# Attention groups of w_in ahead of the retention groups, and finished retention rows transposed by VectorE by way of HBM

## The chip, the cores and the metric

One core of one Trainium2 chip runs the whole kernel. The metric is device time in microseconds (us) of that core, the median of several runs. TensorE is called PE, VectorE DVE, ScalarE ACT, GpSimd POOL, and SyncE SP.

## What is computed

The reference is a network on 256 tokens of width 1024 in fp32: two layers of a first block (DEPTH = 2), then two mixers of a second block. The change touches the mixer of the first block's layers alone:

```python
def hybrid_layer(x, g_mix, w_in, sinks, w_a, w_b, w_out, g_mlp, w_up, w_down):
    h = rmsnorm(x, g_mix)
    z = h @ w_in
    aq, ak, av, rq, rk, rv, rg, ga, gb = jnp.split(z, SPLIT_POINTS, axis=-1)
    aq = rope_half(aq.reshape(B, S, N_Q_HEADS, HEAD_DIM), pos)
    ...
    ya = sliding_window_sink_attention(aq, ak, av, sinks) @ w_a
    rq = retention_rotation(rq.reshape(B, S, RET_HEADS, RET_QK_DIM), pos)
    ...
    r = chunkwise_retention(rq, rk, rv)
    r = r * lax.rsqrt(jnp.mean(r * r, axis=-1, keepdims=True) + EPS)
    r = r.reshape(B, S, RET_V) * jax.nn.silu(rg.astype(jnp.float32))
    yb = r.astype(x.dtype) @ w_b
    mixed = jax.nn.sigmoid(ga) * ya + jax.nn.sigmoid(gb) * yb
    x = x + mixed @ w_out
    h2 = rmsnorm(x, g_mlp)
    x = x + jnp.square(jax.nn.relu(h2 @ w_up)) @ w_down
    return x
```

## The kernel before

Each engine has a program written out by hand, and semaphores join them; each engine works its list strictly in order. The tokens are two tiles of 128 rows (t = 0 and 1).

**Weights** come in pieces of 4 x 128 rows by 512 columns (1 MB; 256 columns for the group AKV). SP loads piece p into one of four raw slots as soon as the piece that used the slot, p-4, is split. A product in fp32 is made of three: ACT writes the rounded upper part (w_hi, `split`, L1485), DVE the remainder (w_lo, L1873). Three slots hold split pieces, so ACT splits p only after PE has used p-3; `step(q)` on ACT and DVE stands for splitting piece q+2. PE's `tokens_out` makes one group of output columns from two pieces into PSUM banks 0 and 1 (OUT, one for each token tile); a bank may be written again when ACT or DVE has evacuated it (`out_free`).

**The twelve groups of w_in** are numbered; group g uses pieces 2g and 2g+1. Before, the order is RQ, RK (retention queries and keys), AQ (attention queries), AKV (attention keys and values), RV0, RV1, RG0, RG1, GA0, GA1, GB0, GB1. In layer 0 the first two groups have programs of their own, `first_group` and `second_group`. Then w_a (pieces A, used for YA), w_b (pieces B, YB), w_out and the MLP follow.

**Windows.** Behind each group g, `window(l, g)` on each engine does what small work of attention and retention has come due: scores of a pair of heads, the turn of probabilities, the products with the values, the retention scores s_ret and s_far, the retention outputs. DVE's `softmax(l, i)` (L1947 to L1966) with ACT's exponentials in its middle serves PE's turn in the next window. On PE the window of group g stands behind the group; ACT and DVE do theirs in round g+1, between the two splits of that round. RG0 and RG1 are evacuated by ACT (tanh) and then DVE (L2131), at the end of their round.

**Rotations.** DVE rotates token tile 0 and POOL tile 1, `rotate_pairs` (L576 to L586) for retention and `rotate_halves` (L600 to L611) for attention. `between` puts a split into the middle of DVE's rotation.

**The trip through HBM.** Rotated rows must be transposed. SP stores them to HBM in one piece (`store_rows`), fetches 32-row blocks on other partitions (`fetch_blocks`), and one DVE instruction transposes all 32 x 32 blocks (`turn_blocks`, L1983). `blocks_moved(l, piece)` places these DMAs in SP's queue behind the load of the given piece. Before, r (the retention rows) goes first and a (the attention rows) later, in two stores.

**The finished retention rows** h_sb (DVE L1977) are transposed before by PE: `turn_rows(h, ...)` (L984), between YA and YB. ACT and DVE then bring them from PSUM into hT_hi and hT_lo.

**turn_vectors** runs once, in layer 0: two small PE transposes, the second of which needs dt_rows, spread by a DVE copy (`spread_dt`, L1937).

## Time and profile before

| | before |
|---|---|
| median of 3 runs | 1015.31 us (1014.49 to 1015.38) |
| profiled execution, its own time | 1015.0 us |
| its span, first to last instruction | 1013.1 us |
| granted TensorE clock, mean | 0.998 |
| PE busy | 1004.5 us (99%) |
| DVE, ACT, POOL busy | 720.8 us (71%), 502.3 us (50%), 170.7 us (17%) |
| HBM read and written | 180.69 MB, 4.72 MB |
| chain that ended last | 93% PE, 3% DVE, 1% each DMA, ACT, issue |

All times within the profile are microseconds from the span's start. Busy shares say who works; whether a wait costs anything is told by what PE does meanwhile. Layer 0 of the first block begins at 0, its layer 1 at about 393 us.

### The profile page before, as it was taken

The numbers are of one execution on the slowest core, as the hardware profiler recorded it, in microseconds if no ns is written. First come the engines' busy times: TensorE is split into PE (matmuls) and PEld (weight loads), VectorE is DVE, ScalarE is ACT, GpSimd is POOL, SyncE is SP. The second block draws the span as 40 slices with busy tenths as digits, with TensorE's granted clock in tenths as the row PEclk, the third lists the DMA queues.
The fourth block names the chain that finished last, engine by engine and source line by source line (L and its number), as shares of the span: only waits on it lengthen the run. The fifth ranks groups of instructions, "written<-read, shape, count | busy, mean of one in ns | idle before, by whom it ended". The sixth has DMA issues, their size and how long they took to land.

```text
span 1013.1 us, 13575 instructions
## 1 busy us (share of the span) xinstructions
PE 1004.5 (99%) x5653; PEld 850.0 (84%) x5653; DVE 720.8 (71%) x817; ACT 502.3 (50%) x616; POOL 170.7 (17%) x129
## 2 busy tenths in 40 slices
PE   9999999999999999999999999999999999999997
PEld 8887788888888888887788888888887899899796
DVE  5878656766565665787765667888877757789974
ACT  6544554454444545454554454444468545654352
POOL 0520000000000000430000020000000149169730
PEclk9999999999999999999999999999999999999999
DMA  9797444555556455596553557555554754345451
GB/s 341 250 288 246 160 155 142 170 180 191 199 176 207 166 178 175 187 294 225 166 167 125 169 147 283 201 177 209 204 170 135 238 178 167 125 166 141 121 188 41
DMA packets 103644, 188.60 MB, mean 186 GB/s; under 512 B 9160, under 2 KB 18464, under 8 KB 103456
## 3 DMA queue, kind: packets, MB, share of 16 engines
q1 hardware_dynamic: 103408, 187.66, 55.8%
q8 instruction: 44, 0.72, 0.3%
q14 instruction: 16, 0.13, 0.0%
q10 hardware_dynamic: 176, 0.09, 0.0%
HBM read 180.69 MB, written 4.72 MB: 183 GB/s over the span
## 4 chain that ended last, share of the span: by engine, by line
PE 93%; DVE 3%; DMA 1%; issue 1%; ACT 1%; SPq 0%; DVEq 0%; ACTq 0%
PE bank L786 13%; PE bank L789 12%; PE bank L788 12%; PE bank L1091 11%; PE bank L811 8%; PE bank L815 7%; PE bank L822 7%; PE bank L1095 6%; PE bank L1173 2%; DVE w_lo L1873 2%; PE bank L984 1%; PE bank L1397 1%; PE bank L968 1%; DMA a_bounce<-arena 1%; PE bank L793 1%; PE bank L803 1%
## 5 line engine op out<-in xcount | busy, mean ns | idle before, releaser
L1873 DVE TENSOR_TENSOR w_lo<-arena,w_hi 128x2048 fp32r<-128x2048 f32 (+1 forms) x80 | 185.1, 2323 | 95.2 <-ACT w_hi L1485 94.8
L1873 DVE TENSOR_TENSOR w_lo<-raw,w_hi 128x2048 fp32r<-128x2048 f32 (+1 forms) x78 | 181.1, 2331 | 80.1 <-ACT w_hi L1485 80.0
L1485 ACT ACTIVATE w_hi<-raw 128x2048 fp32r<-128x2048 f32 (+1 forms) x83 | 157.1, 1892 | 102.3 <-PE bank L789 71.4
L1485 ACT ACTIVATE w_hi<-arena 128x2048 fp32r<-128x2048 f32 (+1 forms) x80 | 151.3, 1892 | 104.6 <-PE bank L789 80.8
L1091 PE MATMUL bank<-hT,w_hi 128*128 128x512 f32 x504 | 123.4, 391 | 0.0
L786 PE MATMUL bank<-w_hi,hT 128*128 128x512 f32 (+1 forms) x296 | 114.1, 385 | 0.9 <-issue 0.9
L1091 PEld LDWEIGHTS bank<-hT,w_hi 128*128 128x128 f32 x504 | 92.2, 188 | 17.6
L2482 POOL TENSOR_TENSOR rstd<-mean,const 128x1 f32<-128x1 f32 (+1 forms) x16 | 9.1, 579 | 528.5 <-DVE mean L1882 359.4
L789 PE MATMUL bank<-w_hi,hT 128*128 128x512 f32 (+1 forms) x256 | 97.9, 382 | 0.0
L788 PE MATMUL bank<-w_lo,hT 128*128 128x512 f32 (+1 forms) x256 | 97.9, 382 | 0.0
L811 PE MATMUL bank<-w_hi,hT 128*128 128x512 f32 (+1 forms) x216 | 83.3, 388 | 0.7 <-DVE arena L2131 0.7
L815 PE MATMUL bank<-w_hi,hT 128*128 128x512 f32 (+1 forms) x216 | 82.0, 382 | 0.0
L786 PE MATMUL bank<-w_hi,uT_hi 128*128 128x512 f32 x192 | 74.9, 390 | 0.0
L789 PE MATMUL bank<-w_hi,uT_lo 128*128 128x512 f32 x192 | 74.7, 389 | 0.0
L788 PE MATMUL bank<-w_lo,uT_hi 128*128 128x512 f32 x192 | 74.7, 389 | 0.0
L1095 PEld LDWEIGHTS bank<-hT,w_lo 128*128 128x128 f32 x504 | 67.0, 191 | 3.9
L1095 PE MATMUL bank<-hT,w_lo 128*128 128x256 f32 x504 | 68.3, 282 | 0.0
L786 PEld LDWEIGHTS bank<-w_hi,hT 128*128 128x128 f32 x296 | 55.6, 188 | 12.3 <-DVE w_lo L1873 1.3
L811 PE MATMUL bank<-w_hi,uT_hi 128*128 128x512 f32 x160 | 62.9, 393 | 0.0
L815 PE MATMUL bank<-w_hi,uT_lo 128*128 128x512 f32 x160 | 62.5, 391 | 0.0
L822 PE MATMUL bank<-w_lo,hT 128*128 128x512 f32 (+1 forms) x216 | 56.1, 381 | 0.0
L788 PEld LDWEIGHTS bank<-w_lo,hT 128*128 128x128 f32 x256 | 48.1, 188 | 9.4
(342 smaller groups left out, 1886.7 us busy)
## 6 DMA issues: line engine op xcount, KB each, us to landing
arena<-in_w_in SPq DMA_DIRECT2D x22, 1024.0 KB, 5.3
raw<-in_w_in SPq DMA_DIRECT2D x20, 1024.0 KB, 5.3
arena<-in_w_up SPq DMA_DIRECT2D x16, 1024.0 KB, 5.3
raw<-in_w_up SPq DMA_DIRECT2D x16, 1024.0 KB, 5.3
arena<-in_w_down SPq DMA_DIRECT2D x16, 1024.0 KB, 5.1
raw<-in_w_down SPq DMA_DIRECT2D x16, 1024.0 KB, 5.1
raw<-in_e_w_in SPq DMA_DIRECT2D x6, 1024.0 KB, 5.1
arena<-in_e_w_in SPq DMA_DIRECT2D x6, 1024.0 KB, 5.1
```

Of the source, the lines that this page charges most:

```text
L786: pe.matmul(dst, a_hi, b_hi, start=first, stop=False, skip_group_check=shared)
L788: pe.matmul(dst, a_hi, b_lo, start=False, stop=False, skip_group_check=shared)
L789: mm = pe.matmul(dst, a_lo, b_hi, start=False, stop=last_one, skip_group_check=shared)
L793: pe.matmul(dst, a_hi, b_lo, start=False, stop=False, skip_group_check=shared)
L811: pe.matmul(dst, a_hi, b_hi, start=(start and i == 0), stop=False, skip_group_check=shared)
L815: pe.matmul(dst, a_lo, b_hi, start=False, stop=False, skip_group_check=shared)
L822: mm = pe.matmul(dst, a_hi, b_lo, start=False, stop=last_one, skip_group_check=shared)
L1091: pe.matmul(UP[j], w_hi[:, s[i], kk, at[j]], hT[:, k, :, :].rearrange("p e t -> p (e t)"), start=(i == kk == 0), stop=False, skip_group_ch ...
L1095: return pe.matmul(UP[j][:, 0:SEQ], w_lo[:, s[i], kk, at[j]], hT_hi[:, i * KP + kk, :], start=False, stop=(i == 1 and kk == KP - 1), skip_ ...
L1173: last = pe.matmul(OUT[t], a[:, KP * i + k, at[t]], w[:, s[i], k, :], start=(first and k == 0), stop=(last_one and k == KP - 1))
L1485: act.activation(w_hi[:, p % SPLIT_RING, :, 0:n], raw_at(p)[:, :, 0:n], copy).then_inc(hi_ready, 1)
L1873: dve.tensor_tensor(w_lo[:, s, :, 0:n], raw_at(p)[:, :, 0:n], w_hi[:, s, :, 0:n].bitcast(F32), ALU.subtract).then_inc(lo_ready, 1)
```

## The change

Four things. (1) The order of the groups of w_in becomes AQ, AKV, RQ, RK, RV0 and so on; the tables of the attention's rotation are loaded ahead of the rest, POOL and DVE rotate attention first, and a is stored and fetched first (one store), r later. (2) The windows move: attention starts in window 4, where it started in 6, the retention scores go to windows 6 to 8 and the retention outputs to windows 8 and 9; some PSUM banks change. turn_vectors moves one group later. (3) The finished retention rows are stored to HBM behind the load of w_b's first piece, fetched in blocks behind its second, and transposed by one DVE instruction, which reads every eighth element (`across`). PE's turn_rows(h) goes, and hT_hi and hT_lo are made from SBUF. (4) The rows of w_b are loaded in the matching order (`across_piece`: each partition takes neighbouring rows). In the diff, cut to its core, ACT's windows and PE's turn and value products, each shifted by two groups, are left out.

```diff
-RQ, RK, AQ, AKV, RV0, RV1, RG0, RG1, GA0, GA1, GB0, GB1 = range(12)
-W_IN_START = (768, 1280, 0, 512, 1792, 2304, 2816, 3328, 3840, 4352, 4864, 5376)
+AQ, AKV, RQ, RK, RV0, RV1, RG0, RG1, GA0, GA1, GB0, GB1 = range(12)
+W_IN_START = (0, 512, 768, 1280, 1792, 2304, 2816, 3328, 3840, 4352, 4864, 5376)
...
+ATT_TABLES = ("att_cos", "att_sin")
...
+        h_moved = area(0, T * BLOCKS, KD * BLOCK)
+        h_raw = area(13312, KD, SEQ)
+        h_bounce = nc.dram_tensor("h_bounce", [T * P, D], F32, kind="Internal").ap()
...
+        def across_piece(w, c, half):
+
+            return w.rearrange("(p k) n -> p k n", p=P)[:, half * KP:half * KP + KP, c * COLS:(c + 1) * COLS]
+
...
 def rotate_halves(eng, o, l, t, tmp, between=lambda part: None):
...
+            between(0)
             o.mark(eng.tensor_tensor(b4[:, :, 0, :], z[:, :, 1, :], sin, ALU.mult))
             o.mark(eng.tensor_tensor(b4[:, :, 1, :], z[:, :, 0, :], sin, ALU.mult))
+            between(1)
             o.settle()
...
+                if n[0] == 3:
+                    sp.dma_start(const[:, FIRST_TABLES:SECOND_TABLES], consts[:, FIRST_TABLES:SECOND_TABLES]).then_inc(att_tables, 16)
                 if n[0] == 4:
                     small_inputs()
-                    sp.dma_start(const[:, FIRST_TABLES:], consts[:, FIRST_TABLES:]).then_inc(const_landed, 16)
+                    sp.dma_start(const[:, SECOND_TABLES:], consts[:, SECOND_TABLES:]).then_inc(const_landed, 16)
...
-                if piece == 12:
+                if piece == 10:
+                    for t in range(T):
+                        sp.wait_ge(rope_done[t], l + 1)
+                    store_rows(a_bounce.rearrange("(t p) n -> p t n", p=P), a_rows, a_stored)
+                if piece == 11:
+                    sp.wait_ge(a_stored, 16 * (l + 1))
+                    fetch_blocks(a_moved, a_bounce, a_blocks)
+                if piece == 13:
                     for t in range(T):
                         sp.wait_ge(rot_done[t], l + 1)
                     store_rows(r_bounce.rearrange("(t p) n -> p t n", p=P), z_ret, r_stored)
-                if piece == 13:
+                if piece == 15:
                     sp.wait_ge(r_stored, 16 * (l + 1))
                     fetch_blocks(r_moved, r_bounce, r_blocks)
-                if piece == 14:
-                    sp.wait_ge(rope_done[0], l + 1)
-                    store_rows(a_bounce[0:P, :], a_rows[:, 0, :], a_stored[0])
-                if piece == 15:
-                    sp.wait_ge(rope_done[1], l + 1)
-                    store_rows(a_bounce[P:2 * P, :], a_rows[:, 1, :], a_stored[1])
-                    for t in range(T):
-                        sp.wait_ge(a_stored[t], 16 * (l + 1))
-                        fetch_blocks(a_moved[:, t * BLOCKS:(t + 1) * BLOCKS, :], a_bounce[t * P:(t + 1) * P, :], a_blocks)
...
-                            load(square_piece(ins[w][l], c, half))
+                            load((across_piece if w == "w_b" else square_piece)(ins[w][l], c, half))
+                            if w == "w_b" and c == half == 0:
+                                sp.wait_ge(r_ready, 2 * l + 2)
+                                store_rows(h_bounce.rearrange("(t p) n -> p t n", p=P), h[:, :, :], h_stored)
+                            if w == "w_b" and c == 0 and half == 1:
+                                sp.wait_ge(h_stored, 16 * (l + 1))
+                                fetch_blocks(h_moved, h_bounce, h_blocks)
...
+                width = AKV_WIDTH
...
-                                last = pe.matmul(OUT[t], a[:, i * KP + kk, at], w[:, s, kk, :],
+                                last = pe.matmul(OUT[t][:, 0:width], a[:, i * KP + kk, at], w[:, s, kk, 0:width],
...
             def window(l, g):
-                if l == 0 and g == 1:
+                if l == 0 and g == 2:
                     turn_vectors()
-                if g == 5:
-                    pe.wait_ge(rT_ready, l + 1)
+                if g == 4:
+                    pe.wait_ge(aT_ready, l + 1)
                     if l == 0:
                         pe.wait_ge(vec_ready, 3)
-                    for n in range(T):
-                        at = slice(n * P, (n + 1) * P)
-                        for hd in range(RET_HEADS):
-                            last = pe.matmul(bank[:, 3 + n, hd * P:(hd + 1) * P], rkT[:, hd, at], rqT[:, hd, at],
-                                             start=True, stop=True)
-                        last.then_inc(s_ret_done, 1)
-                if g == 6:
-                    pe.wait_ge(s_ret_ready, 2 * l + 1)
+                if g in (6, 7):
+                    n = g - 6
+                    if n == 0:
+                        pe.wait_ge(rT_ready, l + 1)
+                    else:
+                        pe.wait_ge(s_ret_ready, 2 * l + 1)
+                    at = slice(n * P, (n + 1) * P)
+                    for hd in range(RET_HEADS):
+                        last = pe.matmul(bank[:, 3, hd * P:(hd + 1) * P], rkT[:, hd, at], rqT[:, hd, at], start=True, stop=True)
+                    last.then_inc(s_ret_done, 1)
+                if g == 8:
...
-                    pe.wait_ge(aT_ready, l + 1)
-                if 6 <= g < 6 + PAIRS:
-                    i = g - 6
+                if 4 <= g < 4 + PAIRS:
+                    i = g - 4
...
-                if g == 10:
+                if g == 8:
...
-                if g == 11:
+                if g == 9:
+                    pe.wait_ge(s_far_ready, l + 1)
                     for hd in range(RET_HEADS):
-                        if hd == 2:
-                            pe.wait_ge(oT_lo, l * PAIRS + PAIRS)
-                        dst = bank[:, (4, 3)[hd // 2], (hd % 2) * RET_V:(hd % 2 + 1) * RET_V]
+                        dst = bank[:, (2, 5)[hd // 2], (hd % 2) * RET_V:(hd % 2 + 1) * RET_V]
...
-                           banks_free=lambda: pe.wait_ge(probsT_odd, l * PAIRS + PAIRS))
-                turn_rows(h, lambda t: r_ready, lambda t, i: 2 * l + t + 1)
+                           banks_free=lambda: pe.wait_ge(r_ready, 2 * l + 2))
...
 def group_out(l, g):
-                if g == RQ:
+                if g == AQ:
...
-                window(l, W_IN_GROUPS - 1)
                 step(p + PIECE_A)
+                act.wait_ge(piece_used, p + 2 * W_IN_GROUPS)
+                act.wait_ge(turned, 4 * (4 * l + 1) + 4)
+                for i in range(4):
+                    act.activation(hT_hi[:, 2 * i:2 * i + 2, :], h_raw[:, 2 * i:2 * i + 2, :], copy).then_inc(turned_hi, 1)
                 step(p + PIECE_A + 1)
-                turn_hi(4 * l + 1)
...
+            def turn_blocks(dst, src, slots, across=False):
+
+                rows_in = src.rearrange("p u (f s) -> p u s f" if across else "p u (s f) -> p u s f", s=slots)
+                return dve.transpose(dst.rearrange("p s (u q) -> p u s q", q=BLOCK), rows_in)
             def window(l, g):
                 if g == 1:
+                    dve.wait_ge(att_tables, 16)
+                    rotate_halves(dve, order, l, 0, z_ga, between=lambda part: step(l * PIECES + 5 + part))
+                if g == 3:
                     dve.wait_ge(const_landed, 16)
-                    dve.wait_ge(sink_landed, 16)
-                    dve.wait_ge(vec_ready, 3)
-                    rotate_pairs(dve, order, l, 0, z_ga, between=lambda part: step(l * PIECES + 2 * AQ + 1 + part))
-                if g == 3:
-                    rotate_halves(dve, order, l, 0, z_ga)
-                if g == 5:
-                    dve.wait_ge(aT_ready, l + 1)
-                    for n in range(T):
-                        dve.wait_ge(s_ret_done, 2 * l + n + 1)
-                        dve.tensor_tensor(s_ret[:, n, :], bank[:, 3 + n, :], tab("decay"), ALU.mult).then_inc(s_ret_ready, 1)
-                if g == 6:
+                    rotate_pairs(dve, order, l, 0, z_ga, between=lambda part: step(l * PIECES + 8 + part))
+                if g in (6, 7):
+                    n = g - 6
+                    dve.wait_ge(s_ret_done, 2 * l + n + 1)
+                    dve.tensor_tensor(s_ret[:, n, :], bank[:, 3, :], tab("decay"), ALU.mult).then_inc(s_ret_ready, 1)
+                if g == 8:
                     dve.wait_ge(s_far_done, l + 1)
                     dve.tensor_tensor(s_far, bank[:, 3, :], tab("decay_far"), ALU.mult).then_inc(s_far_ready, 1)
-                if 7 <= g < 7 + PAIRS:
-                    n = l * PAIRS + g - 7
...
-                if 6 <= g < 6 + PAIRS:
-                    softmax(l, g - 6)
-                if g == 10:
-                    retention_out(l, 0)
+                if g == 4:
+                    dve.wait_ge(sink_landed, 16)
+                if 4 <= g < 4 + PAIRS:
+                    softmax(l, g - 4)
+                if g in (8, 9):
+                    retention_out(l, g - 8)
 
...
                     if g == 4:
-                        window(l, g - 1)
+                        dve.wait_ge(a_blocks, 16 * BLOCKS * (l + 1))
+                        turn_blocks(aT, a_moved, A_SLOTS).then_inc(aT_ready, 1)
+                        dve.wait_ge(aT_ready, l + 1)
                     if g == 6:
-                        dve.wait_ge(a_blocks, 16 * T * BLOCKS * (l + 1))
-                        turn_blocks(aT, a_moved, A_SLOTS).then_inc(aT_ready, 1)
-                    if g == 5:
                         dve.wait_ge(r_blocks, 16 * BLOCKS * (l + 1))
                         turn_blocks(rT, r_moved, 2 * RET_HEADS).then_inc(rT_ready, 1)
-                    if g != AKV and (l or g):
+                    if g not in (3, 4) and (l or g):
                         step(p + 2 * g)
-                    if l == 0 and g == 1:
+                    window(l, g - 1)
+                    if l == 0 and g == 2:
                         spread_dt()
-                    if g != 4:
-                        window(l, g - 1)
-                    if g != AQ:
+                    if g not in (2, 4):
...
-                window(l, W_IN_GROUPS - 1)
+                dve.wait_ge(h_blocks, 16 * BLOCKS * (l + 1))
+                turn_blocks(h_raw, h_moved, KD, across=True).then_inc(turned, 4)
                 for c in range(2):
                     step(p + PIECE_A + c)
                     if c == 0:
-                        retention_out(l, 1)
+                        dve.wait_ge(piece_used, p + 2 * W_IN_GROUPS)
+                        for i in range(4):
+                            dve.wait_ge(turned_hi, 4 * (4 * l + 1) + i + 1)
+                            dve.tensor_tensor(hT_lo[:, 2 * i:2 * i + 2, :], h_raw[:, 2 * i:2 * i + 2, :],
+                                              hT_hi[:, 2 * i:2 * i + 2, :].bitcast(F32), ALU.subtract).then_inc(turned_lo, 1)
                     for t in range(T):
                         gated(c, z_ga, l * USES + USE_YA + c, t, banks=(OUT, YA_BANKS)[c])
-                turn_lo(4 * l + 1)
                 for c in range(2):
...
-            pool.wait_ge(const_landed, 16)
-            pool.wait_ge(vec_ready, 3)
+            pool.wait_ge(att_tables, 16)
             for l in range(DEPTH):
+                rotate_halves(pool, order, l, 1, z_gb)
+                if l == 0:
+                    pool.wait_ge(const_landed, 16)
+                    pool.wait_ge(vec_ready, 3)
                 rotate_pairs(pool, order, l, 1, z_gb)
-                rotate_halves(pool, order, l, 1, z_gb)
```

On DVE, in layer 0, round 2 (the group after the second), the change puts the rotation of the attention rows; L1896 is w_lo of pieces 4 to 9, in order, L613 to L626 is rotate_halves, and L1960 is the copy that turn_vectors needs. Before, at the same place:

```order
L1873 TENSOR_TENSOR w_lo<-arena,w_hi 128x2048 [waits hi_ready]
L1873 TENSOR_TENSOR w_lo<-raw,w_hi 128x2048 [waits hi_ready]
L1937 COPY dt_rows<-log_dt 16x128 [waits ldt_landed]
L1873 TENSOR_TENSOR w_lo<-raw,w_hi 128x2048 [waits hi_ready]
L1873 TENSOR_TENSOR w_lo<-arena,w_hi 128x4x256 [waits hi_ready]
```

And now:

```order
L1896 TENSOR_TENSOR w_lo<-raw,w_hi 128x2048 [waits hi_ready] x2
L1896 TENSOR_TENSOR w_lo<-arena,w_hi 128x2048 [waits hi_ready]
L613 TENSOR_TENSOR arena<-arena,const 128x640 [waits out_free0,att_tables]
L1896 TENSOR_TENSOR w_lo<-arena,w_hi 128x2048 [waits hi_ready]
L617 TENSOR_TENSOR arena<-arena,const 128x10x32
L618 TENSOR_TENSOR arena<-arena,const 128x10x32
L1896 TENSOR_TENSOR w_lo<-raw,w_hi 128x2048 [waits hi_ready]
L624 TENSOR_TENSOR arena<-arena 128x4x2x32 [waits dve_order]
L626 TENSOR_TENSOR arena<-arena 128x64 x2
L624 TENSOR_TENSOR arena<-arena 128x4x2x32
L626 TENSOR_TENSOR arena<-arena 128x64 x2
L1960 COPY dt_rows<-log_dt 16x128 [waits ldt_landed,rope_done0]
```

The copy stood between pieces 4 and 5; it now stands behind piece 8 and the end of the rotation.

On ACT, in layer 0, the second group's evacuation (two rows of L1518) stands behind the w_hi of pieces 4 and 5 as the second group's did before, but it is now AKV's:

```order
L1506 ACTIVATE w_hi<-raw 128x2048 [waits piece_used,raw_landed0,half_ready]
L1506 ACTIVATE w_hi<-raw 128x2048 [waits piece_used,raw_landed1]
L1518 ACTIVATE arena<-bank,rstd 128x256 [waits out0_done]
L1518 ACTIVATE arena<-bank,rstd 128x256 [waits piece_used]
L1506 ACTIVATE w_hi<-arena 128x2048 [waits piece_used,raw_landed2]
```

On DVE, rounds 5 and 6 of a layer (behind RV0 and RV1): w_lo of piece 13, then the transpose of r (L2007), piece 14 and the second softmax, which begins at L1970.

```order
L1896 TENSOR_TENSOR w_lo<-raw,w_hi 128x2048 [waits hi_ready]
L2007 STREAM_TRANSPOSE arena<-arena 128x8x8x32 [waits r_blocks]
L1896 TENSOR_TENSOR w_lo<-arena,w_hi 128x2048 [waits hi_ready]
L2028 COPY arena<-bank 128x384 [waits probs_turned]
L1970 SCALAR_TENSOR_TENSOR arena<-bank,const 128x384 [waits probs_turned,scores_done]
L1970 SCALAR_TENSOR_TENSOR arena<-bank,const 128x384
```

Before, both transposes stood ahead of every softmax of the layer:

```order
L1983 STREAM_TRANSPOSE arena<-arena 128x8x8x32 [waits r_blocks]
L1873 TENSOR_TENSOR w_lo<-raw,w_hi 128x2048 [waits hi_ready] x2
L1983 STREAM_TRANSPOSE arena<-arena 128x8x6x32 [waits a_blocks]
L1873 TENSOR_TENSOR w_lo<-arena,w_hi 128x2048 [waits hi_ready]
L1997 TENSOR_TENSOR arena<-bank,const 128x512 [waits s_ret_done,aT_ready]
L1997 TENSOR_TENSOR arena<-bank,const 128x512 [waits s_ret_done]
L1873 TENSOR_TENSOR w_lo<-arena,w_hi 128x2048 [waits hi_ready]
L2131 SCALAR_TENSOR_TENSOR arena<-arena,bank 128x512 [waits tanh_ready] x2
```

The transpose of r moved from ahead of a's to behind the first softmax.

## Rows read from the trace of the kernel before

**Rows 1.** The page, busy time and share of the span by engine.

```profile
PE 1004.5 (99%) x5653; PEld 850.0 (84%) x5653; DVE 720.8 (71%) x817; ACT 502.3 (50%) x616; POOL 170.7 (17%) x129
```

**Rows 2.** Timeline of ACT, layer 1: start, duration, line; evacuations of tile 1.

```profile
415.10 0.69 ACT L1497 ACTIVATE arena<-bank,rstd 128x512 f32<-128x512 f32 x1 [2.03 <-PE bank L789]
...
425.98 0.69 ACT L1497 ACTIVATE arena<-bank,rstd 128x512 f32<-128x512 f32 x1 [2.03 <-PE bank L789]
...
431.73 0.48 ACT L1497 ACTIVATE arena<-bank,rstd 128x256 f32<-128x256 f32 x1 [0.54 <-PE bank L789]
```

**Rows 3.** Chain that ended last, windows of layer 0: start, duration, what.

```profile
69.58 1.78 PE bank L1015 x16
...
109.09 0.81 PE bank L1051 x6
```

**Rows 4.** The same chain, layer 1, between YA and YB.

```profile
548.95 1.75 PE bank L984 x16
550.69 0.46 issue
```

**Rows 5.** Timelines of SP (stores) and of DVE (block transposes), both layers.

```profile
48.13 0.37 SPq L671 DMA_DIRECT2D r_bounce<-arena  x1
...
62.57 0.67 SPq L671 DMA_DIRECT2D a_bounce<-arena  x1
...
432.03 0.37 SPq L671 DMA_DIRECT2D r_bounce<-arena  x1
...
63.79 2.31 DVE L1983 STREAM_TRANSPOSE arena<-arena 128x2048 f32<-128x2048 f32 x1 [1.67 <-DMA arena<-r_bounce]
...
75.58 1.78 DVE L1983 STREAM_TRANSPOSE arena<-arena 128x1536 f32<-128x1536 f32 x1 [5.11 <-DMA arena<-a_bounce]
...
448.87 2.31 DVE L1983 STREAM_TRANSPOSE arena<-arena 128x2048 f32<-128x2048 f32 x1 [2.86 <-DMA arena<-r_bounce]
```

**Rows 6.** Timeline of DVE, layer 0: rotate_pairs beside POOL.

```profile
33.54 3.42 DVE L576 TENSOR_TENSOR arena<-arena,const 128x1024 f32<-128x1024 f32 x1
...
39.35 2.01 DVE L579 TENSOR_TENSOR arena<-arena,const 128x512 f32<-128x512 f32 x1
```

**Rows 7.** Chain that ended last, layer 0: the second group.

```profile
19.52 11.17 PE bank L968 x48
```

**Rows 8.** Timeline of ACT, layer 0: w_hi of pieces 4 and 5, second group's evacuation.

```profile
25.49 1.92 ACT L1485 ACTIVATE w_hi<-raw 128x2048 fp32r<-128x2048 f32 x1 [3.74 <-issue]
28.09 1.92 ACT L1485 ACTIVATE w_hi<-raw 128x2048 fp32r<-128x2048 f32 x1 [0.68 <-DMA raw<-in_w_in]
29.92 1.50 ACT L1497 ACTIVATE arena<-bank,rstd 128x512 f32<-128x512 f32 x2
```

**Rows 9.** Timeline of DVE, layer 0: second half of rotate_halves, and what follows.

```profile
54.75 0.85 DVE L609 TENSOR_TENSOR arena<-arena 128x256 f32<-128x256 f32 x1
...
57.62 4.49 DVE L1873 TENSOR_TENSOR w_lo<-arena,w_hi 128x2048 fp32r<-128x2048 f32 x2
```

**Rows 10.** Timeline of DVE, layer 1: rotate_pairs beside POOL and without it.

```profile
419.33 2.54 DVE L576 TENSOR_TENSOR arena<-arena,const 128x1024 f32<-128x1024 f32 x1
...
430.71 0.69 DVE L585 TENSOR_TENSOR arena<-arena 128x512 f32<-128x512 f32 x1
```

**Rows 11.** Timeline of DVE, layer 1: first softmax and the split behind it.

```profile
471.52 1.01 DVE L1947 SCALAR_TENSOR_TENSOR arena<-bank,const 128x384 f32<-128x384 f32 x2
...
476.56 1.01 DVE L1966 TENSOR_SCALAR arena<-arena,inv_den 128x128 f32<-128x128 f32 x4
477.95 2.29 DVE L1873 TENSOR_TENSOR w_lo<-arena,w_hi 128x2048 fp32r<-128x2048 f32 x1 [0.39 <-ACT w_hi L1485]
```

**Rows 12.** A stretch: busy time by engine, clock, DMA share, GB/s.

```profile
442.00:444.00 2.00, 2.00 (x10) 1.67 (x9) 2.00 (x2) 1.36 (x2) 0.00 (x0) 1.00 1.14 195
```

**Rows 13.** Line 891, keep_clock: count, duration ns min/median/max, first and last start.

```profile
L891 PE MATMUL bank<-h_sb x18: 421/421/579, 1.0 to 4.8; 128*128 128x128 f32 x18
...
L891 PE MATMUL bank<-const x4: 275/275/275, 6.7 to 7.0; 128*128 128x128 f32 x4
```

71 lines of the change are left out of this document (38 added, 33 removed).

## The prediction

> **What bounds the kernel now.** I read the engines' busy shares first: PE is busy for 99% of the span, VectorE (DVE) for 71%, ScalarE (ACT) for 50% [rows 1]. So the end is PE's work plus every hole in it, and before there are hardly any. Hence two questions: what PE work goes, and where a reordered DVE or ACT now leaves PE without input. For that I use how one w_in group passes. ACT's evacuations of the second row tile of successive groups start 10.88 us apart for a group of 512 columns, 5.75 us for the 256 columns of AKV [rows 2]. The four small attention or retention parts placed between groups cost 0.8 to 0.9 us each (transposes 0.81; scores of one retention tile half of 1.78) [rows 3].
>
> Splitting a weight piece takes ACT 1.91 us (w_hi) and then DVE 2.29 us (w_lo). ACT may start on piece p only when PE has used piece p-3.
>
> **What is saved.** In each layer turn_rows(h) disappears from PE: 16 transpose records, 1.75 us, and the 0.46 us gap behind them [rows 4], 2.21 us; two layers give **-4.4 us**. In their place the h rows go through HBM. That trip has two long groups plus the w_a products to hide in, about 11 + 11 + 11 us, after r_ready, which comes some 5 us into GB0. It needs a store and fetch like that of r (15.7 us between store issue and DVE's transpose in layer 0, 16.8 us in layer 1 [rows 5]), then a 2.3 us transpose, four ACT copies and four DVE subtracts (about 5 us): about 29 of 33 us. I cost it at nothing; the strided read of `across` has no row, and if it ran at the slowest rate of a DVE tensor operation here (512 elements in 2.01 us [rows 6]), it would take 8 us and cost up to 3 us per layer. AKV as second group changes PE's total by nothing.
>
> **Start of layer 0: AKV's evacuation.** Before, the second group starts at 19.5 us [rows 7]. AKV will end at 19.5 + 5.8 = 25.3. The next group needs OUT bank 0, so it waits for AKV's evacuation, which on ACT stands behind the w_hi of piece 5. Piece 5 is bound by its load: pieces 4 and 5 are split at 25.49 and 28.09, which are their landings, 2.6 us per MB [rows 8]. Two half-sized pieces ahead of them save 1 MB, so piece 5 lands at 28.1 - 2.7 = 25.4; w_hi ends at 27.3, the 256-column evacuation at 27.7. PE waits **+2.4 us**.
>
> **Start of layer 0: dt_spread.** turn_vectors now follows RQ and needs dt_spread. On DVE that small copy stands behind the whole rotate_halves, whose last part stands behind w_lo of piece 8. Piece 8 can be split only after PE has used piece 5, that is after RQ. From RQ's end: evacuation 0.65, w_hi 1.85, w_lo 2.3, the second half of the rotation 2.87 (start to start beside POOL [rows 9]; POOL will be done, and I take 2.4), copy 0.2, together **+7.4 us** (6.9 to 7.9). There is no such hole before, because the copy is then a DVE instruction between pieces 4 and 5. PE resumes at about 46.
>
> **Each layer: the serial chain to RG1.** Before, DVE turns r for the window after RV1 and a for the one after RG0, and softmax starts only then. Now DVE must, in one line: wait for a's blocks, turn, rotate retention pairs, store and fetch r, turn, then do the second softmax; only after that comes RG0's evacuation, for which RG1 waits. From the end of rotate_halves:
> - a through HBM: 13.0 us (from the second store's issue to DVE's transpose [rows 5]), turn 1.7;
> - rotate_pairs with pieces 10 and 11 between: 3.4 + 2.3 + 4.0 + 2.2 + 1.3 beside POOL in layer 0 [rows 6]; in layer 1 the first multiply still meets POOL (2.5 [rows 10]) and the rest does not (1.2 for the two next multiplies, 0.69 us each [rows 10]), so 9.5;
> - r through HBM 15.7, turn 2.2, w_lo of piece 14 2.2, probsT 0.5, softmax 6.0 (471.5 to 477.6 [rows 11]), w_lo of piece 15 with its gap 2.6, evacuation 0.6: 29.8.
>
> The sum is 57.7 us in layer 0 and 54.0 us in layer 1. PE's own work over that stretch: in layer 0 from RQ's end and the resumption RK, RV0, RV1 and RG0 (43.5 us) with windows 4 to 6 (0.85 + 1.7 + 3.35 = 5.9), 49.4; the chain started 0.3 us earlier, so PE comes **+8.0 us** late. In layer 1, counted from AQ's start, the rotation ends at about 34.7 (RQ ends at 27.5, plus the 7.2 of the paragraph before) and RG1's bank is free at 88.7; PE alone would be there at 16.6 + 54.4 + 5.9 = 77.0: **+11.7 us**. It shows as waits at windows 4 and 5 and, mostly, at window 6. From then on a DVE round is about 13.3 us (two w_lo, softmax, small copies, evacuation) against PE's 14.2, so the lag isn't repeated, nor recovered.
>
> The unsure term is the HBM trips. Bounds: a from 11 us (one larger store without the second one's wait) to 16.8; r from 14 to 16.8 or somewhat more. While r's blocks come back, the DMA engines are full (share 1.14) at only 195 GB/s [rows 12]. The Trainium skill, "DMA: Bandwidth & Descriptors", opening table, has 512 bytes suffice for line rate; by that the 1 KB packets of the blocks would cost half, and the sum would be about 9 us less over four trips. The row disagrees, and it decides.
>
> **Sum:** -4.4 + 2.4 + 7.4 + 8.0 + 11.7 = +25.1 us. The profiled execution took 1015.0 us around a span of 1013.1, the median of the runs is 1015.3; so about **1040 us**. SP's queue: its waits for a's and r's rotations stand ahead of the loads of pieces 11 and 14, which PE needs over 15 us later, so the queue costs nothing. POOL rotates tile 1 beside DVE and ends before it.
>
> **Rivals.**
> 1. *All of it is covered, and the kernel is faster.* The trips return in time and only the transposes go: 1015.0 - 4.4 = 1010.6. For it: PE is 99% busy, and DVE is idle for some us before both transposes. It decides at window 6: the chain would have to be 12 us shorter in layer 1, and dt_spread would still be in the way. 0.05.
> 2. *Only the start is lost.* Both trips together are 8 to 12 us shorter, nothing is late at window 6: 1015.0 - 4.4 + 2.4 + 7.4 = 1020.4. Against it: four measured trips, none under 13 us. 0.08. A draw near 1015 (half of these) 0.03.
> 3. *The clock falls.* The first 18 records of PE's warm-up matmuls have 421 ns, the same shape a few us later 275 ns [rows 13]: PE begins at 1.2 GHz and is at 2.4 some 5 us later, so that stretch once more costs 2.5 us. After the wait for dt_spread it would hide in the chain. After the 5 us wait of window 6 it would not: 2 x 2.5, 1045. The Trainium skill, "TensorE: Matmul & The Clock Gate", section on the HAM clock gate, has the clock fall after an idle stretch; this profile has no stretch with PE idle for over 1.1 us, so it isn't seen here. 0.28.
> 4. *The h blocks are late too* (the slow strided transpose, 8 us): YB waits up to 3 us per layer, about 1045. 0.10.
>
> **How the numbers follow.** Forecast 0.46 at 1040; its own bounds (trips -3 to +3 us per layer, waits at the start +-1) give 1033 to 1048. Clock and h take the top to 1051; the low end goes down to 1029 for shorter trips than any measured. Faster by over 0.2% (2 us, about what a measurement of this kernel can tell) 0.05, within it 0.03, slower 0.92.
>
> **What would show it.** In the changed profile: a PE wait of 7 us after RQ of layer 0, ended by DVE's dt_rows copy; one of 2 to 3 us before RQ, ended by ACT's AKV evacuation; in both layers DVE idle before both block transposes, a PE wait of 4 to 5 us for the second softmax, and one before RG1 for DVE's evacuation; no transposes of h_sb by turn_rows before w_b. If PE is still 99% busy, the chain is wrong; if the span grows by 10 us only, the trips are; matmuls of 512 columns twice as long behind a wait would be the clock.

## The result, and the profile after it

| | before | after |
|---|---|---|
| median of the runs, us | 1015.08 (4 runs, 1014.49 to 1015.38) | 1053.8 (4 runs: 1050.96, 1051.3, 1056.31, 1056.33) |
| ratio | | 1.0381, 95% interval 1.0345 to 1.0418 |
| profiled execution, us | 1015.0, span 1013.1 | 1056.33, span 1054.5 |
| mean granted clock | 0.998 | 0.978 (0.987 in the two runs of 1051) |

Slower by 38.7 us where 25.1 were forecast. The direction was right; the time is 2.8 us above the upper end (1051) of the range.

The page of the changed kernel, busy time by engine; it answers to [rows 1]:

```profile
PE 1016.0 (96%) x5621; PEld 855.3 (81%) x5621; DVE 719.5 (68%) x811; ACT 501.7 (48%) x616; POOL 173.8 (16%) x129
```

PE has 32 instructions fewer (the transposes of h) and yet 11.5 us more busy time: some of its matmuls ran slowly. The rest are waits. The waits of PE in the changed kernel (engine, tile, line, releaser: us in total, times, longest):

```profile
PE bank L1076 <- DVE arena L1989: 9.9, 4, 3.8
PE bank L1023 <- DVE dt_rows L1960: 6.3, 1, 6.3
PE bank L1056 <- DVE arena L1970: 4.8, 2, 2.4
PE bank L807 <- DVE w_lo L1896: 4.7, 2, 3.1
PE bank L832 <- ACT arena L1518: 3.1, 1, 3.1
PE bank L1042 <- DVE arena L2007: 1.1, 2, 0.5
```

In order of time these are: the AKV evacuation (L832), dt_rows (L1023), windows 5 and 6 of each layer (L1076 for the first and the second softmax; in window 6 also L1042 for the turned retention rows and L1056 for the scores' bank), and the first w_b products behind the h trip (L807). The last was forecast at nothing. Windows of the changed kernel, 5 us each: length, PE busy, PEld, DVE, ACT, POOL, PEclk, DMA share, GB/s:

```profile
25.00:30.00 5.00, 1.94 (x9) 1.56 (x8) 3.69 (x2) 3.68 (x4) 0.94 (x1) 0.80 1.04 386
30.00:35.00 5.00, 5.00 (x13) 3.85 (x12) 4.58 (x3) 0.87 (x1) 5.00 (x3) 0.52 1.04 384
45.00:50.00 5.00, 0.94 (x3) 0.81 (x4) 3.72 (x8) 0.53 (x3) 0.00 (x0) 0.51 0.07 26
50.00:55.00 5.00, 5.00 (x14) 3.84 (x13) 0.00 (x0) 0.00 (x0) 0.00 (x0) 0.50 1.01 339
110.00:115.00 5.00, 4.66 (x17) 3.09 (x17) 5.00 (x4) 2.99 (x4) 0.00 (x0) 0.50 0.41 113
```

The granted clock is at 0.50 to 0.52, the 1.2 GHz level, behind three waits of layer 0: the 3.1 us one before RQ, the 6.3 us one before RK, and those of window 6. RQ takes 13.9 us (28.67 to 42.53) and RK 13.8 us (49.27 to 63.11), instead of 10.9.

DVE's line in layer 0 of the changed kernel, from the attention transpose to RG0's evacuation (start, duration, line, what ended the idle time):

```profile
62.11 1.77 DVE L2007 STREAM_TRANSPOSE arena<-arena 128x1536 f32<-128x1536 f32 x1
63.91 1.22 DVE L589 TENSOR_TENSOR arena<-arena,const 128x1024 f32<-128x1024 f32 x1
65.84 3.71 DVE L1896 TENSOR_TENSOR w_lo<-arena,w_hi 128x2048 fp32r<-128x2048 f32 x1 [0.70 <-ACT w_hi L1506]
69.47 2.02 DVE L592 TENSOR_TENSOR arena<-arena,const 128x512 f32<-128x512 f32 x1
...
98.15 2.31 DVE L2007 STREAM_TRANSPOSE arena<-arena 128x2048 f32<-128x2048 f32 x1 [7.71 <-DMA arena<-r_bounce]
...
111.64 1.28 DVE L2153 SCALAR_TENSOR_TENSOR arena<-arena,bank 128x512 f32<-128x512 f32 x2
```

SP in the same stretch:

```profile
79.50 0.37 SPq L688 DMA_DIRECT2D r_bounce<-arena  x1
79.92 1.60 SPq L683 DMA_DIRECT2D arena<-in_w_in  x2
84.67 1.81 SPq L694 DMA_DIRECT2D arena<-r_bounce  x4
```

Two 1 MB loads stand between the store of the retention rows and the fetch of their blocks. Store to transpose took 98.15 - 79.50 = 18.65 us; in layer 1 it was 20.3 us (store 475.75, transpose 496.01), where [rows 5] had 15.7 and 16.8.

An account of the profiled execution: transposes -4.4 (with their gap); waits before RQ and RK 3.1 + 6.3; RQ and RK slow 3.0 + 3.0. From RK's last evacuation to RG1's start it takes 49.2 us in layer 0 (63.31 to 112.46) and 51.8 in layer 1 (458.50 to 510.33), where PE's three groups and windows 4 to 6 need 3 x 10.88 + 5.9 = 38.5: 10.7 + 13.3. RG1 then runs at half clock for some 4.4 and 2.3 us, which costs about half of it, 2.0 + 1.1. The waits behind the h trip are 1.6 + 3.1 = 4.7. The sum is 42.8, against 41.4 between the spans.

### The profile page after: what moved, and what is told of

It reads as the page before. It is cut to its first block, busy times and chain, and to the rows that moved or that the text cites. A ratio compares the mean times of both kernels' runs of the same rounds, so it can differ in the third digit from the quotient of the medians.

```text
span 1054.5 us, 13515 instructions
## 1 busy us (share of the span) xinstructions
PE 1016.0 (96%) x5621; PEld 855.3 (81%) x5621; DVE 719.5 (68%) x811; ACT 501.7 (48%) x616; POOL 173.8 (16%) x129
## 4 chain that ended last, share of the span: by engine, by line
PE 79%; DMA 8%; DVE 7%; ACT 3%; issue 2%; SPq 1%; DVEq 0%; ACTq 0%
PE bank L807 11%; PE bank L1113 11%; PE bank L809 10%; PE bank L810 10%; PE bank L832 7%; PE bank L836 6%; PE bank L843 6%; PE bank L1117 6%; DVE w_lo L1896 3%; DMA arena<-r_bounce 2%; PE bank L1195 2%; DMA arena<-h_bounce 2%; DMA raw<-in_w_in 2%; ACT w_hi L1506 2%; PE bank L1418 1%
## 5 line engine op out<-in xcount | busy, mean ns | idle before, releaser
L1896 DVE TENSOR_TENSOR w_lo<-arena,w_hi 128x2048 fp32r<-128x2048 f32 (+1 forms) x80 | 188.5, 2365 | 108.1 <-ACT w_hi L1506 107.8
L1896 DVE TENSOR_TENSOR w_lo<-raw,w_hi 128x2048 fp32r<-128x2048 f32 (+1 forms) x78 | 179.2, 2305 | 97.4 <-ACT w_hi L1506 97.3
L807 PE MATMUL bank<-w_hi,hT 128*128 128x512 f32 (+1 forms) x296 | 115.4, 390 | 4.7 <-DVE w_lo L1896 4.7
L809 PE MATMUL bank<-w_lo,hT 128*128 128x512 f32 (+1 forms) x256 | 99.1, 387 | 0.0
L810 PE MATMUL bank<-w_hi,hT 128*128 128x512 f32 (+1 forms) x256 | 98.8, 386 | 0.0
L832 PE MATMUL bank<-w_hi,hT 128*128 128x512 f32 (+1 forms) x216 | 89.2, 414 | 4.0 <-ACT arena L1518 3.1
L836 PE MATMUL bank<-w_hi,hT 128*128 128x512 f32 (+1 forms) x216 | 87.4, 406 | 0.0
L807 PE MATMUL bank<-w_hi,uT_hi 128*128 128x512 f32 x192 | 74.9, 390 | 0.0
L807 PEld LDWEIGHTS bank<-w_hi,hT 128*128 128x128 f32 x296 | 55.9, 189 | 16.9 <-DVE w_lo L1896 5.5
L832 PE MATMUL bank<-w_hi,uT_hi 128*128 128x512 f32 x160 | 62.5, 391 | 0.0
L843 PE MATMUL bank<-w_lo,hT 128*128 128x512 f32 (+1 forms) x216 | 59.2, 397 | 0.0
L810 PEld LDWEIGHTS bank<-w_hi,hT 128*128 128x128 f32 x256 | 48.4, 189 | 9.8
```

Of the source, the lines that this page charges most:

```text
L807: pe.matmul(dst, a_hi, b_hi, start=first, stop=False, skip_group_check=shared)
L809: pe.matmul(dst, a_hi, b_lo, start=False, stop=False, skip_group_check=shared)
L810: mm = pe.matmul(dst, a_lo, b_hi, start=False, stop=last_one, skip_group_check=shared)
L832: pe.matmul(dst, a_hi, b_hi, start=(start and i == 0), stop=False, skip_group_check=shared)
L836: pe.matmul(dst, a_lo, b_hi, start=False, stop=False, skip_group_check=shared)
L843: mm = pe.matmul(dst, a_hi, b_lo, start=False, stop=last_one, skip_group_check=shared)
```

## The experiments

Each time is the median of four runs; the kernel before, measured beside them, had 1015.2 to 1015.5 us. The changed kernel is 1053.8. The difference to it is said each time.

**e1_dt.** The dt_rows copy goes back ahead of the rotation.

```
-                    if l == 0 and g == 2:
+                    if l == 0 and g == 1:
                         spread_dt()
```

> The dt_rows copy of layer 0 moves ahead of the rotation on VectorE, as it stood before. Theory A (one serial line on VectorE, from the rotation of the attention rows to RG0's second softmax, sets when RG1 starts; holes in PE ahead of it in layer 0 hide in it): the 6.3 us wait goes and RK runs at the full clock, but RG1 of layer 0 still starts at about 112 us, waits at windows 4 to 6 grow by what was saved, and the time stays at 1052 to 1056 us. Rival B (every PE wait adds to the end): 6.3 us of wait and 3.1 us of slow clock go, 1043 to 1048 us.

Measured 1043.16 (1041.55 to 1044.27): **-10.6 us**, and theory A fell. The time lies in rival B's range, but not for its reason alone, that every wait adds to the end: the line on DVE itself became shorter. RG1 of layer 0 did not stay at 112 us: RG0's evacuation starts at 100.66 instead of 111.64. The same stretch of DVE in this kernel shows why:

```profile
57.56 1.78 DVE L2007 STREAM_TRANSPOSE arena<-arena 128x1536 f32<-128x1536 f32 x1 [7.09 <-DMA arena<-a_bounce]
59.37 2.55 DVE L589 TENSOR_TENSOR arena<-arena,const 128x1024 f32<-128x1024 f32 x1
61.84 2.28 DVE L1896 TENSOR_TENSOR w_lo<-arena,w_hi 128x2048 fp32r<-128x2048 f32 x1
64.05 0.68 DVE L592 TENSOR_TENSOR arena<-arena,const 128x512 f32<-128x512 f32 x1
```

The line isn't fed by the attention rotation alone; RK's end enters it twice. RK's products free the slot for the split of piece 9, whose w_lo stands ahead of the attention transpose in DVE's order (59.90 in the changed kernel, 48.18 here). And POOL's rotation of the retention pairs starts at RK's evacuation. In the changed kernel that is 64.17, just when DVE does its own, and both crawl: w_lo 3.71 instead of 2.28 us, a 512 element product 2.02 instead of 0.68. Here POOL began 11.8 us earlier and was nearly through. The store of the retention rows left at 68.8 instead of 79.5. Of these 10.7 us, 2.6 are a draw of the clock: in this execution it did not fall after the wait before RQ, though that was 3.3 us long.

**e10_pool.** POOL leaves its rotation of the retention pairs out in layer 0 (tile 1 stays unrotated there), to price that overlap alone.

```
-                rotate_pairs(pool, order, l, 1, z_gb)
+                if l == 0:
+                    ...
+                    pool.tensor_tensor(z_gb[:, 0, 0:P], z_gb[:, 0, 0:P], z_gb[:, 0, 0:P], ALU.mult).then_inc(rot_done[1], 1)
+                else:
+                    rotate_pairs(pool, order, l, 1, z_gb)
```

> The changed kernel without POOL's rotation of the retention pairs in layer 0, which is left out (tile 1 stays unrotated there, so the output is another). Theory A (the late end of RK makes POOL's rotation run beside VectorE's, each slowing the other, and POOL's end at 79 us sets the store of the retention rows): VectorE's five steps and two splits take 9.5 us from 63.9 us on, the store is issued at 73 to 74 us instead of 79.5, RG1 starts 5 to 6 us earlier, 1046 to 1050 us. Rival B (the trip or the slow clock of window 6 sets RG1, not this): store earlier, but time 1052 to 1056 us.

Measured 1045.34 (1041.30 to 1047.43), **-8.5 us**, a little more than theory A had. DVE beside an idle POOL:

```profile
62.60 1.23 DVE L589 TENSOR_TENSOR arena<-arena,const 128x1024 f32<-128x1024 f32 x1
64.53 2.29 DVE L1896 TENSOR_TENSOR w_lo<-arena,w_hi 128x2048 fp32r<-128x2048 f32 x1 [0.69 <-ACT w_hi L1506]
66.73 0.69 DVE L592 TENSOR_TENSOR arena<-arena,const 128x512 f32<-128x512 f32 x1
```

From the end of the attention transpose to the store it is 10.4 us instead of 15.6. The other 3 us can't be put down to POOL with certainty: the retention trip took 18.0 and 18.9 us in this execution, and the clock fell less in RQ.

**e2_fetch.** The fetches go right behind their stores, ahead of the loads.

```
                     store_rows(r_bounce.rearrange("(t p) n -> p t n", p=P), z_ret, r_stored)
-                if piece == 15:
                     sp.wait_ge(r_stored, 16 * (l + 1))
                     fetch_blocks(r_moved, r_bounce, r_blocks)
```

(and alike for a, pieces 10 and 11, and for h ahead of the load of w_b's second piece)

> SP issues each of the three fetches (attention blocks, retention blocks, h blocks) right behind its own store, ahead of the loads that stood between. Theory A (the retention trip took 18.7 and 20.3 us because two 1 MB loads go ahead of the fetch in the queues, and the trip lies on the line that sets RG1): the retention trip falls to 13 to 15 us, the attention trip from 13.3 and 11.4 by up to 2.6, RG1 starts 5 to 8 us earlier in layer 0 and 5 to 8 in layer 1, in all 1040 to 1046 us. Rival B (the blocks come back slowly by themselves, the DMA engines being full at 195 GB/s, and the loads then come late instead): trips within 1 us of what they were, 1050 to 1056 us.

Measured 1041.11 (1039.67 to 1043.02), **-12.7 us**: theory A. The transposes of this kernel:

```profile
89.53 2.31 DVE L2004 STREAM_TRANSPOSE arena<-arena 128x2048 f32<-128x2048 f32 x1 [0.75 <-DMA arena<-r_bounce]
...
481.83 2.31 DVE L2004 STREAM_TRANSPOSE arena<-arena 128x2048 f32<-128x2048 f32 x1 [1.86 <-DMA arena<-r_bounce]
```

With the stores at 77.84 and 469.03 the trips are 11.7 and 12.8 us. DVE's idle time before the transpose falls from 7.7 and 9.3 us to 0.75 and 1.9. The loads that now come later show up as 1.1 us before one group of layer 0 and 0.4 us elsewhere (ACT's w_hi). The waits behind the h trip fall from 1.6 and 3.1 us to 0.8 each, which is part of the 12.7. A part of the 12.7 is the clock again, which fell less in RQ of this execution (0.75 in 30:35 instead of 0.52).

**e3_fill and e5_fill.** Fillers on PE: small matmuls in place of idle time.

```
+                        if l == 0 and g == RQ:
+                            keep_clock(4, 9)
...
+                keep_clock(4, 20)
                 pe.wait_ge(dt_spread, 1)
...
+                    if g == 6:
+                        keep_clock(4, 7)
                     if n:
                         pe.wait_ge(scores_read, n)
...
+                    if g == 6:
+                        keep_clock(4, 11)
                     pe.wait_ge(probs_ready, n + 1)
```

e3_fill had these and, before RG1, 9 more into bank 3 behind a wait for the first retention product.

> PE fills its waits with matmuls of 128 columns into a bank nobody reads: 9 before RQ of layer 0, 20 before the dt_rows transpose, 7 and 11 in window 6 and 9 before RG1, in both layers. No wait goes. Theory A (the granted clock falls after each of these waits and what it costs in front of RQ and RG1 is on the path, about 3 us for RQ and 2 to 2.5 for each RG1, while the 3 us of RK hide in the serial line): 1045 to 1049 us, with the clock at 1.0 in each stretch. Rival B (my prediction: only the waits of window 6 cost clock): 1048 to 1052 us. Rival C (fillers don't hold the clock or the slow matmuls were covered anyway): 1053 to 1057 us.

Measured 1059.7 (1058.2 to 1061.02), **+5.9 us**: none of the three. The fillers before RG1 were the fault. The product that they waited for stands on DVE behind RG0's evacuation, so PE waited for it 5.0 us in each layer and then still had the fillers to do. It prices a badly placed wait and leaves the clock open, hence:

> The changed kernel with fillers of 128 columns on PE once more, now without the ones before RG1, which stood behind a late product of VectorE and so held RG1 back themselves: 9 before RQ of layer 0, 20 before the dt_rows transpose, 7 and 11 in window 6 of both layers. Theory A (the clock that falls after these waits is part of the loss: some 5 us in RQ and RK of layer 0, 3 us behind each window 6): 1044 to 1049 us, clock above 0.99. Rival C (the slow stretches are covered by VectorE's serial line): 1052 to 1056 us.

Measured 1047.11 (1045.85 to 1048.21), **-6.7 us**, theory A. Its windows of the same places:

```profile
30.00:35.00 5.00, 5.00 (x23) 4.11 (x23) 4.58 (x3) 1.39 (x2) 5.00 (x2) 1.00 1.03 372
45.00:50.00 5.00, 3.40 (x11) 2.70 (x12) 1.51 (x8) 0.30 (x2) 0.00 (x0) 0.77 0.55 161
105.00:110.00 5.00, 3.15 (x21) 2.37 (x22) 4.62 (x5) 4.04 (x6) 0.00 (x0) 1.00 0.22 33
```

No cause of a wait was removed, and yet 6.7 us went, with the mean clock at 0.996. The clock still sank in 45:50, where 1.8 us of the dt wait were left unfilled. How much of it is the clock's is best read in layer 0, where the retention trip took the same (18.4 us for 18.7): the first MLP products of that layer start at 235.28 instead of 241.22, 5.9 us earlier. In layer 1 the trip of this execution took 16.7 us instead of 20.3, so that its part is not the clock's alone.

**e4_noh.** The h trip is undone: PE turns the h rows, w_b's rows are loaded as before.

```
-                dve.wait_ge(h_blocks, 16 * BLOCKS * (l + 1))
-                turn_blocks(h_raw, h_moved, KD, across=True).then_inc(turned, 4)
...
+                turn_rows(h, lambda t: r_ready, lambda t, i: 2 * l + t + 1)
```

> The h rows are turned by PE again ahead of w_b, and the h trip and its strided transpose are gone; the rest of the change stays. Theory A (the trip came late by 1.6 us in layer 0 and 3.1 us in layer 1 and so gave back the 4.4 us of the transposes): 1052 to 1056 us, no change. Rival B (my prediction's sum: the trip is hidden and the transposes cost 4.4 us): 1056 to 1061 us.

Measured 1049.67 (1044.49 to 1051.59), **-4.1 us**: below both ranges. Not all of it is the h trip's. What h itself costs stands on PE between w_a's last product and w_b's first. These are w_b's first products of both layers in the changed kernel, then, in this one, the transposes of layer 0 and the product behind them:

```profile
193.96 0.47 PE L807 MATMUL bank<-w_hi,hT 128*128 128x512 f32 x1 [1.56 <-DVE w_lo L1896]
...
592.51 0.47 PE L807 MATMUL bank<-w_hi,hT 128*128 128x512 f32 x1 [3.15 <-DVE w_lo L1896]
```

```profile
190.90 1.91 PE L1000 MATMUL bank<-const,h_sb 128*128 128x128 f32 x16
192.56 0.48 PE L801 MATMUL bank<-w_hi,hT 128*128 128x512 f32 x1
```

In the changed kernel w_a's last products start at 192.00 and 588.98, so from there to w_b's first it takes 1.96 and 3.53 us. Here they start at 190.67 and 582.99 and w_b's first at 192.56 and 584.89, which makes 1.89 and 1.90 us with the transposes. The kernel before has 2.60 us in both layers. So the trip costs 1.7 us more than the transposes do here, nearly all of it in layer 1, and 0.3 us more than the kernel before had in the same place. The rest of the 7.6 us between the two spans lies elsewhere: the retention trip of layer 1 took 16.4 us here instead of 20.3, and the clock behind window 6 of layer 0 was back sooner (0.66 in 110:115 and 1.00 in 115:120, against 0.50 and 0.82).

**e11_h.** The h trip alone is mended: fetch behind the store, and DVE writes its products in the order in which the transpose reads them, so that it isn't strided.

```
+                    last = dve.scalar_tensor_tensor(out=h[:, t, at].rearrange("p (s f) -> p f s", s=KD),
...
-                turn_blocks(h_raw, h_moved, KD, across=True).then_inc(turned, 4)
+                turn_blocks(h_raw, h_moved, KD).then_inc(turned, 4)
```

> The changed kernel with the h trip alone mended: its fetch issued right behind the store, ahead of the load between, and the transpose contiguous. Theory A (the trip costs 4.1 us as it stands, and mended it gains 1.1 us a layer): 6 us less, 1046 to 1050 us, and no wait of w_b's products for VectorE in either layer. Rival B (what the version without the trip gained was a lucky retention trip, 16.3 us instead of 20.3 in layer 1, not the h trip): 1051 to 1054 us, waits of 4.7 us gone or not.

Measured 1048.37 (1047.21 to 1048.80), **-5.4 us**, theory A. DVE in the changed kernel, then in this one:

```profile
178.12 2.29 DVE L1896 TENSOR_TENSOR w_lo<-raw,w_hi 128x2048 fp32r<-128x2048 f32 x1 [2.63 <-ACT w_hi L1506]
181.12 4.16 DVE L2007 STREAM_TRANSPOSE arena<-arena 128x2048 f32<-128x2048 f32 x1 [0.71 <-DMA arena<-h_bounce]
185.18 2.28 DVE L1896 TENSOR_TENSOR w_lo<-arena,w_hi 128x2048 fp32r<-128x2048 f32 x1
```

```profile
175.40 2.29 DVE L1895 TENSOR_TENSOR w_lo<-raw,w_hi 128x2048 fp32r<-128x2048 f32 x1 [2.63 <-ACT w_hi L1505]
177.61 2.30 DVE L2009 STREAM_TRANSPOSE arena<-arena 128x2048 f32<-128x2048 f32 x1
181.35 2.29 DVE L1895 TENSOR_TENSOR w_lo<-arena,w_hi 128x2048 fp32r<-128x2048 f32 x1 [1.45 <-ACT w_hi L1505]
```

The strided read takes 4.16 us against 2.30, and without it and the wait for the blocks DVE has slack again (1.45 us before the next split). Of PE's 4.7 us in L807 a gap of 0.5 us per layer is left, put down to issue. The place between w_a and w_b takes 0.88 and 0.87 us here: 1.0 us a layer less than with the transposes of e4_noh, and 1.7 less than in the kernel before. Against the changed kernel that is 3.7 us; what the median shows beyond it isn't shown to be the h trip's (the retention trip of layer 1 took 18.8 us here, not 20.3). A gap like this one stood behind the transposes before (0.46 us, [rows 4]), but e4_noh, with transposes in the same place, has none; what makes it stays open.

**e6_combo, e8_evac, e7_contig, e9_best.** Combinations. e6 has the dt copy early, both fetches behind their stores, h turned by PE, and fillers before RQ (9) and before the second probability transposes (8). e8 is e6 with ACT evacuating AKV ahead of piece 5's split, and no fillers before RQ:

```
+                    if l == 0 and g == AKV:
+                        group_out(l, g)
+                        step(p + 2 * g + 1)
+                        continue
                     if g != AQ:
```

e7 is e6 with the mended h trip. e9 has e8's order on ACT and the mended h trip; its only fillers are the 8 before the second probability transposes.

> dt_rows copy early, each fetch of attention and retention blocks right behind its store, h turned by PE as before, fillers before RQ (9) and before the second probability transposes (8). Theory A (three separate losses, so their gains add: 10.6, 12.7 and 4.1 us as measured one by one, fillers 2 or 3 more): 1023 to 1027 us. Rival B (dt and the fetches shorten the same line, which is still some 4 us late at RG1 in each layer): 1028 to 1034 us. In neither is it below the kernel before.

> As the combination, without the fillers before RQ, and ScalarE evacuates AKV of layer 0 ahead of the split of piece 5. Theory A (the 3 us wait before RQ is ScalarE's order alone): the wait falls to 0.7 us, 2 to 2.5 us below the combination. Rival B (piece 5's landing at about 26 us then holds RQ's second half or VectorE's rotation): within 1 us of the combination.

> As the combination, but with the h trip kept: fetch right behind the store, VectorE writes its h products already in the order in which a contiguous transpose needs them, so the transpose isn't strided. Theory A (the trip cost 4.1 us only because the fetch stood behind a load and the transpose took 4.17 instead of 2.31 us): no wait before w_b's products, the 4.4 us of the PE transposes are gained, 4 to 5 us below the combination. Rival B (VectorE's strided write or the copies and subtracts between w_a's pieces keep w_b late): equal to the combination or up to 4 us above it.

> All that helped, together: dt_rows early, the three fetches right behind their stores, the contiguous h transpose, ScalarE's AKV evacuation ahead of piece 5's split, fillers (8) before the second probability transposes. Theory A (the h trip gains 1.1 us a layer, the evacuation 2.7 us, and both add): 1024.0 to 1026.5 us. It stays above the kernel before, since VectorE has no idle time left between the two block transposes and RG1 is still 3 to 4 us late in each layer. Rival B (the h trip's gain was the fillers' or the fetches' and doesn't add): 1027 us as the version without the trip.

| kernel | us | beside |
|---|---|---|
| e6_combo | 1029.76 (1029.33 to 1030.22) | 24.0 less than the changed kernel; ratio to before 1.0139 (1.0124 to 1.0154) |
| e8_evac | 1027.07 (1026.20 to 1029.42) | 2.7 less than e6 |
| e7_contig | 1027.86 (1027.27 to 1028.57) | 1.9 less than e6 |
| e9_best | 1024.36 (1023.92 to 1025.71) | 5.4 less than e6; ratio to before 1.0093 (1.0076 to 1.0110) |

e6 bears rival B out: dt and fetches shorten the same line, and their gains do not add (10.6 + 12.7 + 4.1 would be 27.4 without any fillers). e8 bears out theory A, with the L832 wait for the AKV evacuation gone. The h trip gained 1.9 us in e7, between theory A's 4 to 5 and rival B's nothing: mended, it is worth 1 us a layer against the transposes. The two gains of e9 add (2.7 + 1.9 against 5.4). None beats the kernel before. PE's waits in e9:

```profile
PE bank L1075 <- DVE arena L1994: 5.1, 4, 1.7
PE bank L829 <- ACT w_hi L1507: 3.4, 2, 1.7
```

With the two sets of 8 fillers, 2.05 us each, these 8.5 us are 12.6 us of holes; less 3.5 for the transposes of h and their gap that gives 9.1, and e9 is 9.1 above before. All lie in windows 5 and 6 and before RG1, while DVE is idle only 0.67 and 0.81 us before the retention transposes: there the line has become DVE's own work, not the trip.

## Why the prediction was wrong in size

**What held.** PE waited before RQ, for dt_rows and at window 6, each time with the releaser that was named. Before RG1 it waited 0.3 us only, for ACT's w_hi and not for DVE's evacuation. The sum of the retention line behind the transpose was forecast at 14.1 us and took 14.3 (98.15 to 112.46). The first wait was 3.1 for 2.4: piece 5's split began at 26.25 instead of 25.4. The dt wait was 6.3 for 7.4, as the rotation's end took 1.3 us once POOL was through, not 2.4. The attention trip of layer 0, 13.3 us for 13.0, is luck: the split of piece 9, fed by RK's end, stood ahead of the transpose (59.90 to 62.11 on DVE), which shows no wait for the blocks. In layer 1, where DVE did wait for them, it was 11.4 us.

Three steps failed. Their sizes are those of the account of the profiled execution, where the forecast of 25.1 us stands against 41.4 between the spans. They come to 18.1 us for 16.3 missed: the waits at the start were 0.4 less than forecast, and the account itself is 1.4 too high.

**The clock, put at nothing in the sum: 9.1 us.** Rival 3 counted it behind window 6 only, with 0.28; after dt_spread it "would hide in the chain", and the wait before RQ wasn't considered. RQ and RK lost 3.0 us each and RG1 2.0 and 1.1. The clock fell already after the first wait of 3 us, to 0.5 for 6 us or so in two executions, and in e1_dt's not at all. It did not hide, since RK's end feeds the line. e5_fill took 6.7 us off the median, 5.9 of the profiled execution in layer 0. The two levels themselves were read from the durations of [rows 13]; the granted clock of those first us reads 1.00 in that trace.

**"I cost it at nothing", of the h trip, with -4.4 us for the transposes: 4.7 us.** PE waited 1.6 and 3.1 us for it, so that the place between w_a and w_b takes 0.3 us more than before instead of 4.4 less. The fetch stands in SP's queue behind a load that itself waits for the split of piece 23 (issued at 169.56, store at 164.78), and the strided transpose takes 4.16 us; e2_fetch mends the first and has waits of 0.8 us left, e11_h mends both and has none for DVE. Rival 4 had the mechanism, with 8 us for the transpose, and only 0.10.

**The chain to RG1, 24.0 us where 8.0 + 11.7 stood: 4.3 us.** "POOL rotates tile 1 beside DVE and ends before it" is true (78.3 us to 79.5) and misses the point, which is what it does to DVE: 15.6 us to the store instead of 13.2. The retention trip, taken at 15.7 in both layers though [rows 5] has 16.8 for layer 1, was 18.7 and 20.3, above the bound of 16.8 "or somewhat more". In layer 1 the shorter attention trip took 1.6 us of this back, which is luck too. The text saw where the store and fetch go in SP's order, but counted neither load between them; before there was one, now there are two. Of the Trainium skill's 512 bytes for line rate ("DMA: Bandwidth & Descriptors", opening table) I had made 9 us over four trips and set them aside by [rows 12]. The rate did not change: in e2_fetch the blocks still came at 195 GB/s with the engines full (86 to 88 us). But the retention trips were 7.0 and 7.5 us shorter by order alone, which neither the skill's figure nor the row had in it.

**What stays open.** The retention trip of layer 1 varied from 16.4 to 20.3 us between executions that issue it in the same order (16.7 in e5_fill, 18.7 in e1_dt), and the changed kernel's profile has the longest: each single gain above may hold some of that. The two levels of the changed kernel (1051 and 1056 us) differ in clock (0.987 against 0.978 and 0.982), but there is no trace of a 1051 us run, so whether trip or clock makes them was not shown. The single gains overlap and are no split of the 38.7 us.

## What to carry to other kernels

A trip through memory is priced from the issue of its store to the landing of its fetch, and whatever the queue issues between belongs to it: the order of the three fetches was worth 12.7 us here, more than any other single edit. When work is moved onto an engine's serial line, write down every event that feeds the line, not only the first one; the second feeder (RK's end) carried into the line 3 us of slow matmuls that I had declared hidden, and it set POOL's rotation beside DVE's. And a wait on PE like the ones of 3 us here should be costed with the slow stretch that may follow, at half that stretch's length, unless something fills it.

## What the runs showed of the hardware

- DVE beside a working POOL: a 128x2048 split 3.71 us instead of 2.29, a 128x512 product 2.02 instead of 0.69 (e10_pool has both without POOL). The Trainium skill, "GPSIMD Engine Reference", section 1, lists GpSimd's SBUF interfaces as shared with VectorE, with contention for DVE instructions that have two SBUF inputs. The traces agree: these are such instructions, and e1_dt's attention transpose, which has one input, took 1.78 us beside POOL, against 1.77 without it.
- A 32x32 block transpose of 128x2048 that reads its source with a stride of 8 elements: 4.15 to 4.21 us, against 2.31 contiguous. DVE's products written with a stride of 32 elements instead cost 0.13 us each more (four in 2.20 us against 1.66).
- After holes of 3.1 to 3.5 us on PE before RQ the granted clock went to 0.5 for more than 6 us in the changed kernel and e4_noh, for about half of that in e2_fetch, and not at all in e1_dt. The Trainium skill, "TensorE: Matmul & The Clock Gate", section on the HAM clock gate, has the number of slow matmuls at the start of one kernel differ from run to run; these traces show the like behind a hole. Before w_b of layer 1 it was the same: no fall after 3.15 us in the changed kernel, and a fall after 2.98 us in e5_fill (0.86 in 580:585, 0.80 in 585:590). With the fillers in the hole before RQ it stayed at 1.0 in e3_fill, e5_fill, e6_combo and e7_contig.
